# One Trainium2 core: bias and residual of the second product put into all eight banks ahead of it, the bias as a product of two rounded rows

## The reference

```python
a, gate = jnp.split(x @ pw1_w + pw1_b, 2, axis=-1)
u = a * jax.nn.sigmoid(gate)
u = lax.conv_general_dilated(u, dw_w[:, None, :], ...) + dw_b
u = jax.nn.silu(layer_norm(u, ln_g, ln_b))
mix = u @ pw2_w + pw2_b
...
h = layer_norm(DEEPNORM_ALPHA * h + mix, ln_mix_g[i], ln_mix_b[i])
```

## Time and profile before

| | |
|---|---|
| Three runs | 1324.66 us median, 1323.47 to 1326.42 |
| The profiled execution | 1324.57 us, of which the span 1322.4 us |
| PE busy | 1222.5 us (92%) |
| DVE, POOL, ACT busy | 434.9, 272.6, 262.1 us |
| HBM read | 462.09 MB, mean 351 GB/s |
| Chain that ended last, by engine | PE 55%, DMA 34%, DVE 3%, POOL 3% |

### The profile page before, as it was taken

How to read it: one execution, slowest core, us unless ns; L and a number is a source line. 1 busy time by engine, 2 the same in 40 slices (tenths; PEclk the granted TensorE clock), 3 DMA queues, 4 the chain that set the end, 5 groups by cost and what they waited for, 6 DMA issues and landing times.

```text
span 1322.4 us, 15650 instructions
## 1 busy us (share of the span) xinstructions
PE 1222.5 (92%) x6125; PEld 646.8 (49%) x6125; DVE 434.9 (33%) x881; ACT 262.1 (20%) x351; POOL 272.6 (21%) x110
## 2 busy tenths in 40 slices
PE   7999998999798999899899989989998998979895
PEld 7999996587443343243234334323432432343332
DVE  2899998601920221203021220202121121202026
ACT  4665555432310010010001001000100100010001
POOL 5999989187200000000000000000000000000001
PEclk8999998899899999999999989999999999999998
DMA  9766555155679999999999999999999999999993
GB/s 285 214 187 184 165 160 230 61 191 185 260 292 429 428 428 427 427 428 428 429 428 428 428 429 428 428 428 429 428 429 428 428 429 428 428 427 384 424 414 144
DMA packets 102953, 464.73 MB, mean 351 GB/s; under 512 B 4353, under 2 KB 71937, under 8 KB 75265
## 3 DMA queue, kind: packets, MB, share of 16 engines
q1 hardware_dynamic: 102914, 464.20, 87.1%
HBM read 462.09 MB, written 2.10 MB: 351 GB/s over the span
## 4 chain that ended last, share of the span: by engine, by line
PE 55%; DMA 34%; DVE 3%; POOL 3%; issue 2%; SPq 1%; ACT 1%; DVEq 0%; ACTq 0%; POOLq 0%
DMA ring<-in_wu 33%; PE ps L1374 23%; PE ps L1126 12%; PE ps L1231 6%; PE ps L1425 5%; PE ps L1295 4%; POOL ring_r L466 3%; PE ps L1312 2%; DMA xT<-in_xT 1%; SPq L401 1%; PE ps L1171 1%; PE ps L1333 1%; PE ps L1346 1%; PE ps L1164 0%; DVE terms_r L886 0%
## 5 line engine op out<-in xcount | busy, mean ns | idle before, releaser
L1374 PE MATMUL ps<-ring,gain_bias 128*64 128x512 f32 x2048 | 462.4, 606 | 51.8 <-DMA ring<-in_wu 43.7
L1374 PEld LDWEIGHTS ps<-ring,gain_bias 128*64 128x64 f32 x2048 | 158.4, 139 | 349.6 <-issue 349.2
L466 POOL TENSOR_TENSOR ring_r<-ring,ring_r 128x2048 fp32r<-128x2048 f32 x47 | 216.6, 4622 | 62.7 <-ACT ring_r L545 62.7
L1425 PE MATMUL ps<-ring,xT 128*64 128x512 f32 x992 | 219.7, 595 | 4.7 <-DVE xT L1023 4.7
L501 POOL TENSOR_TENSOR rstd<-mv,minus_half 128x1 f32<-128x1 f32 (+1 forms) x3 | 1.8, 600 | 973.9 <-DVE mv L1082 960.8
L1018 DVE TENSOR_TENSOR xT<-xT,ps 128x256 f32<-128x256 f32 x32 | 13.5, 422 | 463.9 <-ACT xT L666 463.9
L771 DVE SCALAR_TENSOR_TENSOR ps<-u,par,ps 128x256 f32<-128x256 f32 x400 | 159.5, 483 | 5.9 <-ACT ps L592 5.9
L1126 PE MATMUL ps<-x_hi,ring_r 128*128 128x272 f32 x1024 | 136.0, 290 | 3.7 <-ACT x_hi L552 3.7
L1425 PEld LDWEIGHTS ps<-ring,xT 128*64 128x64 f32 x992 | 68.5, 137 | 142.6 <-issue 135.3
L1126 PEld LDWEIGHTS ps<-x_hi,ring_r 128*128 128x128 f32 x1024 | 132.3, 190 | 3.9 <-ACT x_hi L552 3.9
L1312 PE MATMUL ps<-xT,pickT 128*128 128x512 f32 x240 | 115.2, 612 | 0.0
(11 more groups left out here) (171 smaller groups left out, 678.4 us busy)
## 6 DMA issues: line engine op xcount, KB each, us to landing
ring<-in_wg SPq DMA_DIRECT2D x62, 2048.0 KB, 15.7
ring<-in_wu SPq DMA_DIRECT2D x62, 2048.0 KB, 20.2
ring<-in_wd SPq DMA_DIRECT2D x62, 2048.0 KB, 16.7
ring<-in_w SPq DMA_DIRECT2D x48, 1024.0 KB, 6.0
ring<-in_wg SPq DMA_DIRECT2D x4, 1024.0 KB, 5.9
ring<-in_wu SPq DMA_DIRECT2D x4, 1024.0 KB, 9.1
ring<-in_wd SPq DMA_DIRECT2D x4, 1024.0 KB, 15.3
xT<-in_xT SPq DMA_DIRECT2D x2, 1088.0 KB, 10.2
```

The source lines that it names most:

```text
L466: nc.gpsimd.tensor_tensor(ring_r[:, lo_slot(c), :], ring[:, raw_slot(c), :], ring_r[:, hi_slot(c), :].bitcast(f32), ALU.subtract).then_inc ...
L1374: mm = nc.tensor.matmul(ps_gu[hh * SLOTS:(hh + 1) * SLOTS, :].rearrange("p (a f) -> p a f", a=2), xgT[:, 4 * m + c, q, :], ring[:, s:s + 3 ...
L1425: mm = nc.tensor.matmul(ps_y[g * SLOTS:(g + 1) * SLOTS, nb, :], midT[:, f % 2, (f // 2) * SLOTS:(f // 2 + 1) * SLOTS], ring[:, s, g * 1024 ...
```

## The change

The bias row is split into two rounded rows. It is loaded as 128 x 16 (`b2_cols`) in place of one row; ACT writes the rounded part and, between tiles 3 and 4, a rounded pair of rows of ones (`ones_r`); DVE writes the rest after tile 4; SP copies both parts by DMA into two rows of `gain_bias_r`, which lies over the old tile, ahead of the loads of chunks 32 to 35. `prime_bias` is then one f32r matmul over two rows.

POOL does the four `shift_tiles` as soon as the shift is there, 8 tiles ahead of the last `pool_sum` and 6 behind it, and `low(34)`, which stood ahead of them, behind all. ACT squares tile 14 third, and does `high(35)` behind that.

On TensorE the four bias products that stood behind the provisional mean go to the x products of their banks, between the groups of squares. Banks 4 and 5 are primed right after banks 6 and 7, ahead of the second product, with a wait on `var_in` and two more float32 products into bank 4, whose result the priming overwrites.

```diff
-SQUARED = ((0, 4), (4, 8), (8, 12), (12, 14), (14, 15), (15, 16))
+SHIFTED = ((0, 4), (4, 8), (8, 12), (12, 14))
+SQUARED = ((0, 4), (4, 8), (14, 15), (8, 12), (12, 14), (15, 16))
...
+        gain_bias_r = under("gain_bias_r", [P, 2, D])
+        b2_rows = gain_bias_r[0:2, 1, :]
...
-            sp.dma_start(b2_row, b2).then_inc(b2_s, 16)
+            sp.dma_start(b2_cols[:, :], b2.rearrange("o (p k) -> (o p) k", k=KT)).then_inc(b2_s, 16)
             with sp.Fori(1, KT // 4) as i:
                 pw1_chunks(i)
+            sp.wait_ge(b2_lo, 1)
+            for part in range(2):
+                sp.dma_start(b2_rows[part:part + 1, :].bitcast(f32).rearrange("o (p k) -> o p k", k=KT),
+                             b2_parts[:, part, :].bitcast(f32)).then_inc(b2_rows_s, 16)
...
-            low(W1_CHUNKS + 2, 2)
-            shift_tiles(0, 4)
+            for a, b in SHIFTED[:2]:
+                shift_tiles(a, b)
             pool_sum(KT - 1, 3)
-            for a, b in SQUARED[1:4]:
+            for a, b in SHIFTED[2:]:
                 shift_tiles(a, b)
-            for n in range(W1_CHUNKS + 3, W_CHUNKS):
+            for n in range(W1_CHUNKS + 2, W_CHUNKS):
                 low(n, n % 4)
...
+            act.wait_ge(consts, N_CONSTS)
+            nc.scalar.activation(ones_r[:, :], ones[0:2, :], ACT.Copy)
+            act.wait_ge(b2_s, 16)
+            nc.scalar.activation(b2_parts[:, 0, :], b2_cols[:, :], ACT.Copy).then_inc(b2_hi, 1)
...
-                if c == 0:
+                if c == 2:
                     high(W1_CHUNKS + 3, 3)
...
+                if tile == 4:
+                    dve.wait_ge(b2_hi, 1)
+                    nc.vector.tensor_tensor(b2_parts[:, 1, :], b2_cols[:, :], b2_parts[:, 0, :].bitcast(f32),
+                                            ALU.subtract).then_inc(b2_lo, 1)
...
-                nc.tensor.matmul(ps[:, bank, :], ones[0:1, :], b2_row[:, bank % 4 * 512:(bank % 4 + 1) * 512],
+                nc.tensor.matmul(ps[:, bank, :], ones_r[:, :], b2_rows[:, bank % 4 * 512:(bank % 4 + 1) * 512],
                                  start=True, stop=False)
...
-            pe.wait_ge(b2_s, 16)
-            for bank in (0, 1):
-                prime_bias(bank)
+            pe.wait_ge(b2_rows_s, 32)
...
+            pe.wait_ge(var_in, 1)
+            for _ in range(2):
+                nc.tensor.matmul(ps[:, 4, :], ident_alpha[:, :], h[:, 0, 0:512], start=True, stop=True)
+            for bank in (4, 5):
+                prime_bias(bank)
+                mm = prime_x(bank)
+            mm.then_inc(primed, 1)
...
-                if step_k == PW2_LEAD - 1:
-                    prime_rest()
```

More of the change, by code:

```diff
@@ L113, in build @@
         ident_alpha = sb("ident_alpha", [P, P])
-        b2_row = bias[0:1, :]
+        b2_cols = sb("b2_cols", [P, KT])
+        b2_parts = sb("b2_parts", [P, 2, KT], f32r)
+        ones_r = sb("ones_r", [2, P], f32r)
         before = sb("before", [P, P], bf16)
@@ L211, in build @@
         kept = sem("kept")
+        b2_hi, b2_lo, b2_rows_s = sem("b2_hi"), sem("b2_lo"), sem("b2_rows_in")
         shift_ps, shifted = sem("shift_ps"), sem("shifted")
@@ L615, in _ @@
             for c, (a, b) in enumerate(SQUARED):
-                if c < 4:
-                    act.wait_ge(centred, c + 1)
+                if (a, b) in SHIFTED:
+                    act.wait_ge(centred, SHIFTED.index((a, b)) + 1)
                 else:
-                    act.wait_ge(taps, a * TILE_OPS + DVE_TAPS + (3 if c == 4 else 2))
+                    act.wait_ge(taps, a * TILE_OPS + DVE_TAPS + (3 if a < KT - 1 else 2))
                 nc.scalar.activation(squares[:, a:b, :], conv[:, a:b, :], ACT.Square).then_inc(squared, 1)
-                if c == 0:
+                if c == 2:
                     high(W1_CHUNKS + 3, 3)
@@ L1184, in _ @@
             nc.tensor.matmul(ps_shift, mean_w[:, :], total_c, start=True, stop=True).then_inc(shift_ps, 1)
-            pe.wait_ge(b2_s, 16)
-            for bank in (0, 1):
-                prime_bias(bank)
+            pe.wait_ge(b2_rows_s, 32)
             pe.wait_ge(made, KT)
-            for bank in (2, 3):
-                prime_bias(bank)
             squares_part(0)
@@ L1196, in _ @@
             for bank in (2, 3):
+                prime_bias(bank)
                 prime_x(bank)
-            squares_part(2)
             pe.wait_ge(shifted, 1)
             mean_part(KT - 2)
-            squares_part(3)
-            squares_part(4)
+            for c in range(2, 5):
+                squares_part(c)
             mean_part(KT - 1).then_inc(sums, 1)
@@ L1207, in _ @@
                 prime_x(bank)
-            def prime_rest():
-                pe.wait_ge(var_in, 1)
-                for bank in (4, 5):
-                    prime_bias(bank)
-                    mm = prime_x(bank)
-                mm.then_inc(primed, 1)
+            pe.wait_ge(var_in, 1)
+            for _ in range(2):
+                nc.tensor.matmul(ps[:, 4, :], ident_alpha[:, :], h[:, 0, 0:512], start=True, stop=True)
+            for bank in (4, 5):
+                prime_bias(bank)
+                mm = prime_x(bank)
+            mm.then_inc(primed, 1)
             def pw2_part(t, k):
```

## The result

Over 20 runs of each on one chip the changed kernel took 1322.62 us (median, 1319.64 to 1326.67), the kernel before 1325.68 us (1322.41 to 1330.24): a ratio of 0.9976, with a 95% interval of 0.9967 to 0.9985, or 3.2 us, between 2.0 and 4.4. The forecast was 1318.7, 5.9 us faster. So the direction was right and the measured time lies in the range, but the forecast gain was about twice what came.

The account below looks back on a forecast made before the run. TensorE was taken to bound the kernel from the squares through the second product, gains there carrying to the end. Reaching low(36)'s reader at 258.15 instead of 264.06 gains 5.9: 1324.57 - 5.9 = 1318.7 us, range 1316.0 to 1322.8.

Parts of the forecast that it names:

- Squares start: TensorE's first squares, ahead of the sums: to start at 215.03 instead of 218.09, 3.06 us earlier.
- From the sums to a free TensorE: Last square, banks 6 and 7, extra x products, banks 4 and 5: 7.6 us, TensorE free at 237.3.
- the wait at k = 4: In the second product, TensorE waits 2.4 us for POOL's low(36), held by SiLUs and high(36); continues at 258.15, not 264.06.
- the low clock at the squares: After TensorE restarts with the squares, a low clock as before costs 1.6 us, bounds 0 and 3.4.
- The pair: One two-row bias product plus one x product on TensorE: 1.36 us, between 1.09 and 2.1.
- The clock in the new wait: Second product: the wait of 2.4 us may bring the clock down, costing 1.7 us and leaving 4.2 gained.
- Forecast A: Second product capped by the SiLUs, clock stays up: 5.9 us gained, 1318.7 us; chance 0.45.
- B: Second product capped by the SiLUs, but the clock falls: 4.2 us gained, 1320.4 us; chance 0.36.
- The reference: Kernel before, one execution: third part of k = 4 in the second product reached at 264.06, the base for 5.9 gained.
- C: Bias priming: two-row product no cheaper than one-row, pairs of 2.1 us; gain 2.4, 1322.2 us; chance 0.08.
- D: At the sums, low clock and switches vanish and DVE's last tile bounds: gain 8.5, 1316.1 us; chance 0.06.
- E: Clock falls before the priming and stays down at the one-row price: 5.8 us later, 1330.4 us; chance 0.05.

Follow-up runs that it names:

- e1: Changed kernel with ACT's high(36) ahead of the last four SiLUs: 1321.40 us, ratio to the kernel before 0.9967.
- e9: As e5, with a rounded 128-row product in each place between the squares where the changed kernel has a two-row one: 1321.57 us, ratio 0.9964.
- e5: Changed kernel with the bias products of banks 0 to 3 moved into TensorE's idle time ahead of the squares: 1319.18 us, ratio 0.9955.
- e12: Repeat of e5, bias products of banks 0 to 3 ahead of the squares in the changed kernel: 1321.08 us, ratio 0.9955.
- e6: Changed kernel with both the bias move of e5 and the earlier high(36) of e1: 1315.94 us, ratio 0.9932.
- e15: Repeat of e6, both moves in the changed kernel: 1316.85 us, ratio 0.9933.
- e7: Kernel before with only the orders of POOL's subtractions and ACT's squares changed: 1325.61 us, ratio 0.9991.
- e4: Changed kernel run again without any edit: 1324.94 us, ratio to the kernel before 0.9996.

## Why the prediction was right or wrong

**The mechanism was right.** Squares start 4.94 us after the provisional mean (forecast 4.96). From the sums to a free TensorE: 7.5 us (7.6). ACT has no pause ahead of `high(36)`, and the wait at k = 4 is on POOL's `low`: 1.81 us (2.4). Part of the difference is TensorE's pace: the third part of k = 4 comes 18.83 us behind the product's start where nothing holds it (e1), not 18.4. What was gained at the end of the product reached the experts' DMA and the end nearly whole: 5.81 us at the last matmul, 5.33 at the DMA, 4.8 at the end. These three contain the 1.77 us by which the provisional mean stood earlier.

**The step that failed: the low clock at the squares.** The prediction said "The same again costs half of that, 1.6 us; bounds are 0 and 3.4". It took the length of the low stretch from the kernel before, where squares alone stood in it, although the change puts two-row products there. In four of seven executions with these squares it lasted over 11 us, half of which is 5.6 us and not 1.6, and the product started 3.3 to 3.8 us later than in the changed kernel's first execution. That it lasted so long is read from the traces; what held it down is open, as said above. The upper bound, 3.4, was half of the longest stretch in that trace, and the changed kernel went beyond it. The trace held a warning that I read only as history: the clock fell at 234.9 while TensorE was busy with one-row and x products.

**The pair** was forecast at 1.36 and took 1.43; four ahead of the sums, 0.3 us. With the squares' clock as forecast the mean is read 20.10 us after the provisional mean, where 19.63 was forecast and 20.81 had been: 0.7 gained instead of 1.1. The rule cited from the Trainium skill (TensorE: Matmul & The Clock Gate, Part 3: Packing small matmuls), weight loads overlapping only where row groups differ, would have given 1.6 for the pair by the prediction's estimate. The measured value lies between that and the 1.19 of a pair of equal rows in e9; so these rows show some added time, less than the rule gives.

**The clock in the new wait.** Forecast A, that it stays, had 0.45, B, that it falls, 0.36. The profiled execution is B: gained in the stage 4.04 against 4.2 forecast. Over eight executions it fell three times, at 1.6 us (forecast 1.7). Choosing A was no error of the sum, but as a mean it overstates the gain by 0.6.

**The reference was high, as far as two executions tell.** 264.06 for the third part of k = 4 contained a low stretch in the priming (from 248.5 on) that the second execution of the kernel before doesn't have, 1.75 us in the product and 1.4 in the stage. One execution stood for the kernel.

**Together.** The stage averages 124.3 in the two executions of before and 121.5 in the three of the changed kernel, 2.8 us, beside 3.2 (2.0 to 4.4) in the times. The forecast of 5.9 loses about 0.7 for the reference and 0.6 for the falls behind the wait, which leaves 1.4 to 1.8 for the squares. As a check, 3.3 to 3.8 us in four of seven executions make 1.9 to 2.2. The split rests on few executions and is an estimate. That the profiled execution came near to the forecast is luck: it had the short low clock at the squares and was set against the longer of the two stages of before.

**Rivals.** C (the two-row product as dear as the one-row one) is out: 0.42 to the next start against 1.05. D did not occur: DVE still waited 3.51 us for the mean. Its 3.7 us at the sums would not have reached the product whole either: with the mean read at 17.45 to 18.55 us after the provisional mean (e5, e12, e9, e6, e15, e7) the product started at 26.9 each time, behind `low(35)`. The prediction put this `low` at 231.3, wanted at 250, and did not ask what DVE does beside it. In the changed kernel it ended at 229.49 and DVE's subtraction began at 229.66, so it cost nothing there. E did not occur in the changed kernel, but its core, a clock that stays down while small-row products are among the work, is what happened, at the squares and not in the priming.

## What to carry to other kernels

A matmul of two rounded rows is a cheap way to add a bias, but it is better put into TensorE's idle time than between the products of a path that has just come out of idle: there the clock stayed at its low level for over 11 us in five of eight executions. Where a foreign piece is taken out of a stream, ask which producer is late next: here `high` and `low` stood behind SiLUs that nothing needed yet, and moving one instruction ahead of four others was worth about as much as the whole change (3.5 us in e1 against e4, 3.2 in e6 against e5). Ask the same of the engine beside the path: once the sums came early, POOL's `low` of a chunk wanted some 20 us later set the start of the product. And a term that depends on the clock needs bounds for the new mix of instructions, and more than one execution of the kernel before.

## What the runs showed of the hardware

With TensorE recorded as busy throughout, the granted clock stayed at 0.50 for 11.1 to 14.8 us after the squares had started in five executions with two-row products among them, and 2.9 to 4.5 us in nine without; the rows are not shown to be the reason. DVE's subtraction of 128x256, 0.41 us in eleven executions, took 1.67 to 2.77 us in the six in which it began while POOL's `low(35)` ran, and ended 0.28 us behind it each time. A two-row product beside an x product cost 0.24 us more than a 128-row one in the same place (1.43 against 1.19 a pair). And POOL's `low(36)` took 5.49 us in e6, where it runs beside DVE's last groups, 4.78 in e1, and 4.57 in the changed kernel, where it starts behind them. DVE's rounding of 128x1024 took 4.11 us beside it in e6, against 0.69 in the changed kernel (e6, then the changed kernel):

```profile
251.03 4.11 DVE L838 CAST xT_r<-conv 128x1024 fp32r<-128x1024 f32 x1 [0.93 <-ACT conv L645]
```

```profile
250.16 0.69 DVE L836 CAST xT_r<-conv 128x1024 fp32r<-128x1024 f32 x1 [0.28 <-ACT conv L643]
```

That the two engines held each other up is inferred from the overlap. The 0.24 us that TensorE waits in e6 is less than the 0.92 by which its `low(36)` is longer.
